# A mixture-of-experts kernel: three small experts with high and low parts in one stationary operand

## The reference, cut to what matters

```python
def swiglu(h, w1, w3, w2):
    return (jax.nn.silu(h @ w1) * (h @ w3)) @ w2

def moe_ffn(h, router_w, router_b, w1, w3, w2):
    logits = h.astype(jnp.float32) @ router_w.astype(jnp.float32) + router_b.astype(jnp.float32)
    top_v, top_i = lax.top_k(logits, TOP_K)
    top_w = jax.nn.softmax(top_v, axis=-1)
    combine = jnp.sum(jax.nn.one_hot(top_i, N_EXPERTS, dtype=jnp.float32) * top_w[..., None], axis=-2)
    ...
    for e in range(N_EXPERTS):
        y = y + combine[..., e:e + 1] * swiglu(h, w1[e], w3[e], w2[e])
    return y
```

## Time and profile before

| | us |
|---|---|
| median of three runs (1536.78 to 1537.92) | 1537.56 |
| span of the profiled execution, first to last instruction | 1535.7 |
| TensorE busy | 1515.2 |
| VectorE busy | 1298.2 |
| ScalarE busy | 968.0 |
| GpSimd busy | 90.3 |

### The profile page before, as it was taken

How to read it: one execution, slowest core, us unless ns; L and a number is a source line. 1 busy time by engine, 2 the same in 40 slices (tenths; PEclk the granted TensorE clock), 3 DMA queues, 4 the chain that set the end, 5 groups by cost and what they waited for, 6 DMA issues and landing times.

```text
span 1535.7 us, 19169 instructions
## 1 busy us (share of the span) xinstructions
PE 1515.2 (99%) x7785; PEld 1236.0 (80%) x7785; DVE 1298.2 (85%) x1175; ACT 968.0 (63%) x841; POOL 90.3 (6%) x141
## 2 busy tenths in 40 slices
PE   8999999999999999999999999999999999999997
PEld 4886799999788568888888888888888888888885
DVE  5888887778885579988899999898998888998996
ACT  3532444444554357777777777787777787777775
POOL 5300100000000030100000100000010000000000
PEclk9999999999999999999999999999999999999999
DMA  9776698877823199999999999999999999999990
GB/s 347 285 254 239 231 359 323 304 288 274 310 94 131 55 312 391 377 385 386 354 363 385 369 392 391 354 364 382 367 390 376 376 357 375 382 364 372 411 368 30
DMA packets 161862, 494.13 MB, mean 322 GB/s; under 512 B 4587, under 2 KB 8855, under 8 KB 161767
## 3 DMA queue, kind: packets, MB, share of 16 engines
q1 hardware_dynamic: 156160, 474.76, 82.7%
q0 software_dynamic: 4928, 16.69, 3.1%
q10 hardware_dynamic: 678, 1.40, 0.2%
HBM read 483.91 MB, written 8.91 MB: 321 GB/s over the span
## 4 chain that ended last, share of the span: by engine, by line
PE 90%; DVE 6%; SPq 2%; DMA 1%; ACT 1%; issue 0%; DVEq 0%; ACTq 0%
PE bank L1323 20%; PE bank L1324 20%; PE bank L1325 20%; PE bank L975 4%; PE bank L1183 4%; PE bank L1224 3%; PE bank L1223 3%; PE bank L1222 3%; PE bank L972 2%; PE bank L1356 2%; PE bank L1198 1%; PE bank L1199 1%; PE bank L1200 1%; DMA ring<-in_w_mod_dram 1%; DVE ring_low L2044 1%; PE bank L998 1%
## 5 line engine op out<-in xcount | busy, mean ns | idle before, releaser
L2044 DVE TENSOR_TENSOR ring_low<-ring,w_high 128x2048 fp32r<-128x2048 f32 x336 | 768.6, 2293 | 95.1 <-ACT w_high L2547 89.0
L2547 ACT ACTIVATE w_high<-ring 128x2048 fp32r<-128x2048 f32 x336 | 646.6, 1926 | 228.8 <-PE bank L1325 220.3
L1323 PE MATMUL bank<-w_high,x_high 128*128 128x512 f32 x896 | 352.9, 394 | 0.1
L1324 PE MATMUL bank<-ring_low,x_high 128*128 128x512 f32 x896 | 351.4, 392 | 0.0
L1325 PE MATMUL bank<-w_high,x_low 128*128 128x512 f32 x896 | 348.9, 389 | 0.0
L1323 PEld LDWEIGHTS bank<-w_high,x_high 128*128 128x128 f32 x896 | 168.5, 188 | 37.4 <-DVE ring_low L2044 1.2
L1325 PEld LDWEIGHTS bank<-w_high,x_low 128*128 128x128 f32 x896 | 168.2, 188 | 37.4
L1324 PEld LDWEIGHTS bank<-ring_low,x_high 128*128 128x128 f32 x896 | 168.3, 188 | 34.7
L1323 PE MATMUL bank<-w_high,act_high 128*128 128x512 f32 x448 | 178.8, 399 | 0.2 <-DVE ring_low L2044 0.2
L2468 ACT ACTIVATE tmp_r<-ring 128x1024 fp32r<-128x1024 f32 x84 | 88.9, 1061 | 140.8 <-PE bank L1224 82.0
L1324 PE MATMUL bank<-ring_low,act_high 128*128 128x512 f32 x448 | 177.7, 397 | 0.0
(11 more groups left out here) (381 smaller groups left out, 1657.3 us busy)
## 6 DMA issues: line engine op xcount, KB each, us to landing
ring<-in_moe_w_dram SPq DMA_DIRECT2D x168, 2048.0 KB, 9.1
ring<-in_w_mod_dram SPq DMA_DIRECT2D x23, 2048.0 KB, 12.9
ring<-in_ffn_w_dram SPq DMA_DIRECT2D x21, 2048.0 KB, 11.8
ring<-in_w_in_dram SPq DMA_DIRECT2D x7, 2048.0 KB, 13.6
ring<-in_w_out_dram SPq DMA_DIRECT2D x4, 2048.0 KB, 8.4
ring<-in_w_in_dram SPq DMA_DIRECT2D x4, 1024.0 KB, 15.5
ring<-in_w_mod_dram SPq DMA_DIRECT2D x2, 1024.0 KB, 15.7
gate_row<-in_b_mod_dram POOLq DMA_DIRECT2D x4, 512.0 KB, 7.6
```

Of the source, the lines that this page charges most:

```text
L1323: mm(out_, x_h, w_h, start=first, stop=False)
L1324: mm(out_, x_h, w_l, start=False, stop=False)
L2044: tt_(moe_low(u, m // 2)[:, c], moe_slot(u, m // 2)[:, c], w_high[:, m % HIGHS, :].bitcast(F32), ALU.subtract).then_inc(low_made, 1)
L2547: act(w_high[:, m % HIGHS, :], moe_slot(u, m // 2)[:, c], ACT.Copy).then_inc(high_made, 1)
```

## The change

Experts 0 and 1 stay first. The other six are ordered by the number of their tokens, counted on the chip (`later_order`, on VectorE, in the first expert). The three with the most tokens become the first of the pairs 1 to 3, the three with the fewest the second: experts 3, 5 and 7 in the order of work (`is_small`). SyncE reads the number of each later expert from memory and loads from a computed address.

A small expert has 64 slots (SMALL). Its gathered tokens stand twice in the 128 columns of the stationary operand: the first 64 columns get the high parts, the other 64 the low parts. One matmul with w_high and one with ring_low then do what three did, and rows 0 to 63 and 64 to 127 of a result have to be added. For gates and values that is done in the turn: ScalarE copies both banks to act_s and act_m, and TensorE multiplies each 128 x 128 piece with `fold`, two identities of 64 above each other, in full four-byte form, instead of transposing the product. Silu, product, rounding and subtraction then have 256 columns for a group, and act_high holds high and low side by side. The result rows are added in DRAM: two scatters, of which the second adds. If one of the three has more than 64 tokens, the rest goes to the second run.

```diff
+        def is_small(q, g, u):
+            return q == 0 and g > 0 and u == PAIR - 1
+        def rows_before(r):
+            return r + sum(is_small(0, n // PAIR, n % PAIR) for n in range(r))
...
-                    if q == 0 and c == 2 * NCH:
-                        eng.wait_ge(route_v.sem, route_v.at("most_i"))
+                    if q == 0 and c == FIRST * NCH:
+                        eng.wait_ge(perm_v.sem, perm_v.at("order"))
...
+                    if later and i == 0:
+                        number_of = eng.value_load(order_i[0:1, e - FIRST:e - FIRST + 1], min_val=0, max_val=NE - 1)
...
-            for n in range(2 * TT):
+            for n in range(2 * TT + 1):
                 eng.dma_start(expert_rows[n * P:(n + 1) * P, :], y_low.bitcast(F32)).then_inc(s_zero, 16)
...
+                if is_small(0, g, u):
+                    eng.indirect_dma_start(expert_rows[:, :],
+                                           bass.IndirectOffsetOnAxis(index[:, g % 2, 0, u, PAIR:PAIR + 1], 0),
+                                           rows, None, bounds_check=2 * T + P - 1,
+                                           oob_is_err=False).then_inc(s_rows_out, 16)
+                    eng.wait_ge(s_rows_out, 16 * (rows_before(r) + 1))
+                    eng.indirect_dma_start(expert_rows[:, :],
+                                           bass.IndirectOffsetOnAxis(index[:, g % 2, 0, u, PAIR + 1:PAIR + 2], 0),
+                                           rows, None, bounds_check=2 * T + P - 1, oob_is_err=False,
+                                           compute_op=ALU.add).then_inc(s_rows_out, 16)
...
                 def three(out_, x_h, x_l, w_h, w_l, first, last):
+                    if small_one:
+                        mm(out_, x_h, w_h, start=first, stop=False)
+                        return mm(out_, x_h, w_l, start=False, stop=last)
...
                 def turn(j):
+                    if small_one:
+                        eng.wait_ge(s_const, N_CONSTS + LATE_CONSTS)
+                        eng.wait_ge(even_a.sem, even_a.at(f"q{j}", small_rep(g)))
+                        for n, part in enumerate((act_s, act_m)):
+                            for hb in range(HB):
+                                c = n * HB * SMALL + hb * SMALL
+                                ins = mm(bank[6 + j % 2][:, c:c + SMALL], part[:, j % 2, hb * P:(hb + 1) * P], fold,
+                                         start=True, stop=True)
...
                         if m == 9 and not first and not q:
-                            eng.wait_ge(s_rows_out, 16 * r)
+                            eng.wait_ge(s_rows_out, 16 * rows_before(r))
...
+                        if first and 6 <= m < 13:
+                            later_order(m - 6)
...
+                    def small_products(*js):
+                        for j in js:
+                            eng.wait_ge(moe_a.sem, moe_a.at(f"s{j}", r))
+                            done(eng, tt_(act_m[:, j % 2, 0:HB * SMALL], act_s[:, j % 2, 0:HB * SMALL],
+                                          bank[6 + j % 2][:, HB * SMALL:], ALU.mult).then_inc(moe_v.sem, 1),
+                                 moe_v, f"m{j}", r)
+                        for j in js:
+                            eng.wait_ge(moe_a.sem, moe_a.at(f"ah{j}", r))
+                            done(eng, tt_(halves_of(j)[:, :, SMALL:], folded(act_m, j),
+                                          halves_of(j)[:, :, 0:SMALL].bitcast(F32), ALU.subtract).then_inc(moe_v.sem, 1),
+                                 moe_v, f"al{j}", r)
...
+                    def small_highs(*js):
+                        for j in js:
+                            eng.wait_ge(moe_t.sem, moe_t.at(f"t{j}", r))
+                            done(eng, act(act_s[:, j % 2, 0:HB * SMALL], bank[6 + j % 2][:, 0:HB * SMALL],
+                                          ACT.Silu).then_inc(moe_a.sem, 1), moe_a, f"s{j}", r)
+                        for j in js:
+                            eng.wait_ge(moe_v.sem, moe_v.at(f"m{j}", r))
+                            done(eng, act(halves_of(j)[:, :, 0:SMALL], folded(act_m, j), ACT.Copy).then_inc(moe_a.sem, 1),
+                                 moe_a, f"ah{j}", r)
...
+                        if m in (10, 18, 30, 38) and small_one:
+                            j = 2 * (10, 18, 30, 38).index(m)
+                            for n in range(j, min(j + 2, NJ)):
+                                copy_value(n)
```

More of the change, by code:

```diff
@@ L126 @@
 FIRST_CONSTS = 10
+SMALL = SLOTS // 2
+FIRST = 2
+LATER = NE - FIRST
+N_SMALL = NE // PAIR - 1
 DVE_K = 5
@@ L206 @@
         ("lgt lg max0 eq0 cand0 first0 pick0 lg2 max1 eq1 cand1 first1 pick1 sel diff ch1 ch0 one w1 w2 sw1 sw2 wt ch2 "
-         "most most_i idle row0 row1 token0 token1").split(),
+         "count idle row0 row1 token0 token1").split(),
+    "perm_v":
+        ("key less rank lot over pos some count most most_i hot at order_f order sel2 at0 put0 at1 put1 row0 row1").split(),
+    "even_a":
+        ("p0 p1 q0 q1 p2 p3 q2 q3 p4 p5 q4 q5 p6 q6").split(),
     "route_a":
@@ L1416, in one_expert @@
                 if is_first(q, g, u):
-                    eng.wait_ge(route_v.sem, route_v.at("most"))
+                    eng.wait_ge(route_v.sem, route_v.at("count"))
                 up(0, "w3", 2)
@@ L2197, in experts @@
                         two_experts(q, g)
[L2198 removed]
+                weight = choice[:, PAIR, 2, :] if q else ordered[:, 2, LATER - 1, :]
                 if q == 0:
@@ L2535, in fill_high @@
                     k = slice(first, first + n)
-                    done(eng, act(x_high[:, u, k, :], x_slots[:, k, u, :], ACT.Copy).then_inc(fill_a.sem, 1),
+                    slots = slice(0, SMALL if small_one else SLOTS)
+                    done(eng, act(x_high[:, u, k, slots], x_slots[:, k, u, slots], ACT.Copy).then_inc(fill_a.sem, 1),
                          fill_a, f"h{u}{name}", rep)
```

222 lines of the change are left out of this document (178 added, 44 removed).

## The result

The changed kernel takes **1545.0 us** (median of 4 runs, 1542.7 to 1548.2) against 1537.7 us for the kernel before (4 runs, 1536.8 to 1538.5). The ratio is 1.0057, with a 95% interval of 1.0039 to 1.0074: slower by 7 us by the medians and by some 9 us by the ratio, beyond the 0.2% that such a measurement can resolve. The forecast was 1541.7 us, and its sum of +4.1 us is 3 us short of the medians' difference.

What follows compares the result with a forecast made beforehand. The prediction took TensorE to bound the kernel, with VectorE and DMA close behind. Terms of -13.1, +12.8, +3.4 and +1.0 summed to +4.1 us, a forecast of 1541.7 us for the median, range 1522 to 1558.

Steps and rivals of the forecast that it cites:

- What bounds before: In the kernel before, TensorE bounds at 119 us an expert; at most about 14 us of 121 can be had.
- the next pair's tokens: On ScalarE in a small expert that ends a pair: x_slots and x_high in six intervals add 4.5 us.
- Small experts, -13.1: Experts 3, 5 and 7: 4 us less each for 3 and 5, 5.1 less for 7, together -13.1 us.
- The loop's sum: Small expert ending a pair: ScalarE and VectorE's loop with its extra work takes 117.1 us against 121.2.
- the places where the engines answer each other: Four places per small expert where ScalarE and VectorE wait in turn: three of 3.44 us, one of 3.0, 13.3 in all.
- One sign that was named: Experts 3 and 5 would take 117 us from scatter to scatter, with ScalarE nearly without a gap.
- The added wait, +12.8: Experts 4 and 6: VectorE waits for two scatters in a row, idling TensorE 6.4 us each, +12.8 us.
- The clock, +3.4: Behind each stall in experts 4 and 6 TensorE's clock halves for 3.40 us, losing 1.7 us: +3.4 us.
- The first expert, +1: Some 24 small VectorE operations ordering the experts, behind half chunks 6 to 11, add 1 us, from 0 to 4.
- the second scatter is as good as free: Rival for experts 4 and 6: both scatters land in time and nothing is lost, 1525.5 us; chance 0.10.
- the clock falls in the small experts: Rival: TensorE, busy for 80% only, loses clock once at each of twelve places, 20 us, giving 1562; chance 0.15.
- The sum: Whole kernel: the terms -13.1, +12.8, +3.4 and +1.0 give +4.1 us, a median of 1541.7 us.

Runs made afterwards that it cites:

- own_three: own_buffer with a third product put back in experts 3, 5 and 7 (that with the weights' low part done twice): 1572.0 us, ratio 1.0228.
- own_later: own_buffer with the small experts' rounding and subtraction behind the fold one half chunk later on both engines: 1521.8 us, ratio 0.9895.
- before_twice: The kernel before with a second, plain scatter writing the same rows again for experts 3 and 5, and waits for both: 1555.1 us, ratio 1.0125.
- before_add: The kernel before with a second, adding scatter of the same rows for experts 3 and 5, and waits for both: 1558.0 us, ratio 1.0143.
- hold_clock8: The changed kernel with 8 plain products that change no result ahead of half chunk 10 in experts 4 and 6: 1545.4 us, ratio 1.0052.
- own_buffer: The changed kernel with rows of experts 3 and 5 scattered from the free xn, VectorE waiting only at half chunk 26: 1526.4 us, ratio 0.9936.
- own_one_product: own_buffer with one matrix product in place of two per weight block in experts 3, 5 and 7, the weights' low part left out: 1534.1 us, ratio 0.9972.
- one_scatter: The changed kernel without the adding scatter of experts 3 and 5, whose rows are left out of the result: 1525.8 us, ratio 0.9933.

## Why the prediction was right, and where its terms were off

The direction, the range and the mechanism held: small experts a little shorter, experts 4 and 6 longer by a wait for the scatters, TensorE no longer the bound in the small ones. That the number comes within 3 us owes something to luck, as the last point shows. Point by point:

- **What bounds before.** Held. The forecast gave TensorE "some 92 us" in a small expert; own_three's 132.7 less 38.4 gives 94. (The forecast's own terms, 115.3 - 38.4 + 11 and 1.5 for the next pair's tokens, give 89.)
- **Small experts, -13.1.** The ledger has -10.9 (3.5, 2.6, 4.8). The loop's sum gave 117.1 us; measured were 117.67 and 118.60. The largest term, the places where the engines answer each other, three of 3.44 us and one of 3.0, is in VectorE's timeline of expert 3 to within 0.02 us:

```profile
955.60 0.87 DVE L2247 TENSOR_TENSOR act_m<-act_s,bank 128x256 f32<-128x256 f32 x2
956.63 0.89 DVE L2252 TENSOR_TENSOR act_high<-act_m,act_high 128x256 fp32r<-128x256 f32 x2 [0.16 <-ACT act_high L2765]
959.04 4.64 DVE L2182 TENSOR_TENSOR ring_low<-ring,w_high 128x2048 fp32r<-128x2048 f32 x2 [1.53 <-ACT w_high L2718]
```

From product to next half chunk these are 3.44 us, and the other three places have 3.45, 3.43 and 2.98. But own_later shows that taking the second answer away gives less than 1 us an expert back by itself, so the term is the length of these places and not what they cost. The term for the next pair's tokens is added up wrongly: 8 x 0.59 + 1.5 - 6 x 0.38 is 3.9 and not 4.5. What the sum leaves out is the clock, which was low for 3.4 us in expert 3 and for 6.8 in expert 5. One sign that was named failed: ScalarE is not nearly without a gap, but busy for 96.2 of 118.6 us in expert 5 (the stretch shown beside own_later's), and VectorE for 102.7.
- **The added wait, +12.8.** The step that was mis-sized most: 8.73 and 8.70 us instead of 6.4, within its bounds of 5.1 to 9.3. The point from which the stall counts held: TensorE wants half chunk 10 16.1 us after the scatter, and it ran dry 16.16 us after (1051.27 to 1067.43). VectorE's place held too: it was at its product 12.2 us after the scatter, and 12.1 before (the 13.7 us of the forecast count from the gated half, 1.5 us ahead of the scatter). What was off is the landing of the second scatter: forecast 9.3 + 9.3 + 0.9 = 19.5 us after the first was issued, measured 21.8, and these 2.3 us are the whole error of the stall. The 21.8 are 9.25, then 0.76 until GpSimd issues again, which the forecast had at nothing, then 11.80 in place of 10.2, of which GpSimd itself takes 3.66 where it takes 2.33 for the first. A plain second scatter took 10.0 and not 9.3 in before_twice, the adding one 11.4 in before_add and 11.7 to 11.8 here.
- **The clock, +3.4.** 1.65 and 2.2 us of slow half chunk in the profile, 3.9 in all, although the clock was low for 6.8 and 10.2 us and not 3.4: the rest fell into the stall, where no work was to be done. So the size is in part luck, two and three times the length with more than half of it free. hold_clock8 confirms it in the profile (2.8 of it back), not in the times.
- **The first expert, +1.** 2.5 us in the profile, of which 1.85 are there already when the routing begins (VectorE's logits_t at 548.24 instead of 546.40). Two stretches of the changed kernel tell why (PE, PEld, DVE, ACT, POOL busy, clock, DMA share, GB/s):

```profile
126.80:130.20 3.40, 3.40 (x12) 1.65 (x9) 3.22 (x6) 1.23 (x2) 0.00 (x0) 0.50 1.05 400
553.50:556.90 3.40, 2.94 (x19) 2.11 (x19) 2.95 (x7) 1.09 (x3) 0.00 (x0) 1.00 0.79 318
```

The kernel before is the other way round, with 0.50 at 553.50 and the full clock at 126.80:

```profile
126.80:130.20 3.40, 3.40 (x8) 1.53 (x9) 3.22 (x6) 1.23 (x2) 0.00 (x0) 1.00 1.06 401
```

Where and how often the clock falls ahead of the logits differs from profile to profile, though none of the experiments touches that part: logits_t starts at 544.7 to 545.4 us in four kernels with no stretch at 0.50 ahead of it, at 546.1 to 546.7 in five with 3.4 us of it, at 548.2 in two with 6.8, and at 551.6 and 553.0 with 13.7 and 17.1. From the logits to the first scatter, own_buffer takes 146.90 us against 144.71 of the kernel before, both with one stretch at 0.50 in it; the changed kernel takes 145.39 against 143.21 of before_twice, both without. So the term should have been 2.2 us and not 1.
- **The rivals.** That the second scatter is as good as free was wrong as the kernel is, and right once nobody waits for it (own_buffer). The Trainium skill's figure for such a DMA, in "DMA: Bandwidth & Descriptors", section "Anatomy of one DMA - SWDGE (gpsimd) path", an estimate of 3.2 us, doesn't agree with any landing of a scatter here, 9.0 to 11.8 us beside the ring's transfers. That the clock falls in the small experts happened in five places for 3.4 us each, of the twelve that this rival had; by the table above a place costs 0.5 to 1.3 us and not 1.7, an estimate of some 4 us in all. own_one_product shows the rival at work once TensorE has still less to do.
- **The sum.** Terms of -13.1, +12.8, +3.4 and +1.0 against -10.9, +17.4, +3.9 and +2.5, with 2.2 us gained elsewhere (0.9 in experts 1 and 2, and 0.6 to 0.7 in each of experts 4 and 6 outside the stall; why the large experts got shorter wasn't examined): +10.7 of span, +7.3 of the medians. All four terms erred to the same side, by 8.8 us together. That the median is only 3 us over the forecast comes from the 2.2 us of the large experts, which no term had, and from the profiled execution being 3.2 us slower than the median.

## What to carry to other kernels

When a transfer is doubled, look for who waits for its source to come free, and how much of the present cover is used up: here 2.9 us of spare cover (12.2 less 9.3) met 12.5 us more of landing. The cheapest repair was neither a faster nor a smaller transfer, but another buffer that happened to be free, which turned a loss of 7 to 9 us into a gain of 10 with the same traffic. And when the bound engine's work is cut by a third, expect the gain to stop at the next loop, a few per cent on: here 38 us fewer products, of which the fold's turns took 12 back, gave 3 to 5 us an expert, and cutting further made the kernel slower. Before two profiles are compared to a microsecond, count the stretches at the lower clock in both.

## What the runs showed of the hardware

- The landing of the adding scatter follows GpSimd's own time for it, which isn't constant: 3.66 us in the changed kernel with a landing after 11.8, 1.57 us in own_buffer with 10.2, at the same point of the program. Less that time the 20 adding scatters of all profiles land after 7.8 to 8.7 us, the two plain second ones of before_twice after 7.2 (10.25 less 3.09, 9.82 less 2.62), and the 91 others, all plain, after 6.7 to 8.3, mostly 7.0 (9.25 less 2.33 is 6.9). So adding is worth about 1 us, and what makes GpSimd's share vary by 2 us wasn't found.
- GpSimd issued the second scatter 0.76 us after the first had landed, in each of the 22 cases.
- Two scatters of 0.5 MB that nobody waits for cost nothing beside loads at 400 GB/s: own_buffer and one_scatter differ by 0.6 us.
- The granted clock falls after a stretch in which TensorE is idle or thinly used, and the price is only what it has to do before the clock returns: 1.65 and 2.2 us of 6.8 and 10.2 us at 0.50. With one product of three in own_one_product it fell again and again, and expert 3 took 5.5 us more than with two (124.3 against 118.8 us).
- Each 3.4 us at 0.50 cost 1.4 to 1.7 us ahead of the logits (by the starts of logits_t over all 13 profiles) and 1.5 us in the first expert (146.90 against 145.39 us). Executions of one and the same kernel differ in the same way: of 15 of the kernel before the one with a mean clock of 0.992 took 1542.2 us, and those with 0.998 took 1534.1 to 1535.3.
